# Sparse attention of the odd layer: from per-head items in seven blocks to one block on pairs of heads

## The chip, the cores and the metric

The kernel runs on one core of a Trainium2 chip. Its time is the device time of one execution in microseconds; before the change it is 2824.45 us, the median of three runs (2823.25 to 2824.95). Engines: PE (TensorE), PEld (its weight loads), DVE (VectorE), ACT (ScalarE), POOL (GpSimd), SP (SyncE, which issues most transfers).

## The reference

Two transformer blocks over 256 tokens of width 1024, one after the other; everything is float32. The second block has an even layer (differential attention, state-space mixer, feed-forward) and an odd layer. The odd layer's first half is the place of the change:

```python
q, kc, vc, ksl, vsl, kwn, vwn, gl, cq, ckv, kr = split_cols(h @ od_w_in[i], ODD_SPLITS)
c_out = nsa_attention(q, kc, vc, ksl, vsl, kwn, vwn, gl, ...)     # 8 heads of 64, 2 key groups
d_out = mla_attention(cq, ckv, kr, ...)                           # 4 heads
x = x + concat([c_out, d_out]) @ od_w_out[i]
x = x + moe_swiglu(rms_norm_2(x, od_norm_ffn[i]), ...)            # 8 experts, 2 per token
# inside nsa_attention, for each block of 128 queries and each head:
ck = rope(rms_norm(silu((blocks_of_32(kc) + pos) @ w1[0]) @ w2[0]))   # 15 compressed keys a group
cv = silu((blocks_of_32(vc) + pos) @ w1[1]) @ w2[1]                   # 15 compressed values
o_c = (softmax(mask(q @ ck)) * valid) @ cv
o_s = softmax over the selected blocks' keys (ksl, vsl), causal
o_w = softmax over a window of 512 (kwn, vwn), causal
out = g0 * o_c + g1 * o_s + g2 * o_w                                  # sigmoid gates of gl
```

With 256 tokens there are four blocks of 64 keys, fewer than the 16 that the selection takes, and the window of 512 is wider than the sequence. Both the selected and the window branch are therefore plain causal attention over 256 keys, each on keys and values of its own.

## The kernel before

Tokens lie on the 128 partitions in two tiles (t = 0, 1). Work is written as blocks: inside a block each engine runs its own list of instructions and waits on semaphores, and all engines meet at a block's end. A chained DVE instruction is waited for before the next is issued. `p.ps[i]` is PSUM bank i. A float32 product shows in the records as two PE instructions, a float32 transpose as one.

`linear` (L868) computes the odd layer's projection into `proj` from a stream of 1 MB weight chunks. Beside it POOL runs `nsa_heads` (L1976), norm and rotary embedding of queries and of the two key sets; ACT issues the loads of the compression weights (L270). `nsa` (L1989) then runs block after block:

- `nsa_compress` (L1901): `turn` (L801, transposes on PE, copies by DVE and ACT) of the keys and values to compress, on 64 partitions; then one block for both kinds in turn: position adds on DVE (L1930), 32 products of 64x64 by 30 columns (both groups side by side, L1953), the activation by ACT's exponential and three DVE operations (L1934 to L1936), the second product (L1960); norm and rotary embedding of the compressed keys; a `turn` of them.
- a `turn` of queries and keys: every head's 64 features on partitions 0 to 63.
- `attention` (L1206) on 16 items (head, t) of the compressed branch: scores (L1238), mask added, maximum, scale (L1271, L1273, L1278), exponential with accumulated sum (L1304), validity product (L1282), transpose (L1246), copy (L1312), values (L1256), reciprocal and output (L1289, L1290).
- `attention` on 32 items (branch, head, t); an item has 128 keys for t = 0 and 256 for t = 1, so two items make a cycle.
- a block of the gates: sigmoid, then per tile three products of 512 columns and two sums (L2039 to L2041).

`mla` (L2045) follows, then the output projection, routing and the experts. Another attention of the kernel, `block1_attention` (L1368), works on pairs of heads: two heads' features on partitions 0 to 63 and 64 to 127, scores of the pair into two banks (L1453), maxima on DVE (L1541, L1542), exponentials (L1512), transposes (L1463), copies (L1506), values with a column of ones that yields the sum (L1477), output (L1556 to L1561). Its three calls, on 512, 256 and 512 keys, are in the trace.

## Time and profile before

| | |
|---|---|
| median of 3 runs | 2824.45 us |
| the profiled execution | 2822.43 us, span 2820.7 us |
| PE busy | 2485.3 us (88%) |
| DVE busy | 1855.9 us (66%) |
| ACT busy | 1334.9 us (47%) |
| POOL busy | 204.7 us (7%) |
| granted TensorE clock, mean | 0.910 |
| HBM traffic | 191 GB/s over the span |

Busy times are sums over the span. The granted clock is the share of full speed that the throttle let TensorE have; it is 1.00 at 2.4 GHz and 0.50 at 1.2 GHz, and a stretch with a number between had both. In lines of the timeline the first number is the start in us, the second the time from first start to last end of the merged instructions, and the bracket is the idle time before with what ended it.

### The profile page before, as it was taken

Reading aid. Unit: us, or ns where it says so; the run is one execution under the profiler, and the core shown is the slowest. Engines: PE = TensorE matmul, PEld = TensorE weight load, DVE = VectorE, ACT = ScalarE, POOL = GpSimd, SP = SyncE. Lnnn points to the kernel's source line nnn. Section 1 sums busy time; section 2 is a strip of 40 time slices with the busy share of each in tenths; the row PEclk is TensorE's granted clock in tenths of the full one; section 3 lists DMA queues with packets and bytes.
Section 4 is the critical chain, followed back from the end, with each engine's and each line's share of the span. In section 5 each row is a group of like instructions: output and inputs, shape, how many; then the busy total and the mean of one; then the engine's idle time right before and its main releaser. Section 6 shows DMA issues by size and latency. Waiting matters only on the chain. (4 is left out here: it accounts for less than half of the span.)

```text
span 2820.7 us, 45360 instructions
## 1 busy us (share of the span) xinstructions
PE 2485.3 (88%) x17186; PEld 2233.7 (79%) x17186; DVE 1855.9 (66%) x3132; ACT 1334.9 (47%) x2140; POOL 204.7 (7%) x181
## 2 busy tenths in 40 slices
PE   7888999899978899795389985937899999999998
PEld 5877897789877789794389974626899999999997
DVE  3645555555564555656755552665899999999897
ACT  2343433443344344422144431303677777777776
POOL 0500000000013000071000032000000000000000
PEclk9999999999989999895589985558999999999999
DMA  8604554445531345340045440002799999999995
GB/s 322 253 16 182 214 215 151 165 174 215 194 107 44 132 172 191 126 150 0 0 150 187 172 169 15 1 0 83 287 344 328 342 343 327 341 343 333 329 344 219
DMA packets 82041, 541.75 MB, mean 192 GB/s; under 512 B 9328, under 2 KB 9776, under 8 KB 33840
## 3 DMA queue, kind: packets, MB, share of 16 engines
q1 hardware_dynamic: 79184, 529.57, 50.9%
q10 hardware_dynamic: 2656, 9.40, 0.9%
q8 instruction: 139, 2.28, 0.3%
q14 instruction: 62, 0.51, 0.1%
HBM read 537.88 MB, written 1.05 MB: 191 GB/s over the span
## 5 line engine op out<-in xcount | busy, mean ns | idle before, releaser
L843 PE MATMUL bank<-w_hi,src_hi 128*128 128x256 f32 x2304 | 671.8, 292 | 15.3 <-DVE src_lo L614 4.4
L2471 DVE TENSOR_TENSOR w_lo<-ring,w_hi 128x1024 fp32r<-128x1024 f32 x528 | 637.7, 1221 | 61.3 <-ACT w_hi L2407 41.8
L844 PE MATMUL bank<-w_lo,src_hi 128*128 128x256 f32 x2304 | 653.1, 283 | 0.0
L845 PE MATMUL bank<-w_hi,src_lo 128*128 128x256 f32 x2304 | 652.3, 283 | 0.0
L843 PEld LDWEIGHTS bank<-w_hi,src_hi 128*128 128x128 f32 x2304 | 441.3, 192 | 39.2 <-issue 30.4
L844 PEld LDWEIGHTS bank<-w_lo,src_hi 128*128 128x128 f32 x2304 | 442.0, 192 | 12.1 <-issue 6.7
L845 PEld LDWEIGHTS bank<-w_hi,src_lo 128*128 128x128 f32 x2304 | 442.1, 192 | 0.0
L843 PE MATMUL bank<-src_hi,w_hi 128*128 128x256 f32 x1472 | 426.8, 290 | 12.7 <-DVE w_lo L1150 8.9
L1150 DVE TENSOR_TENSOR w_lo<-ring,w_hi 128x1024 fp32r<-128x1024 f32 x264 | 322.8, 1223 | 169.5 <-ACT w_hi L1087 169.3
L844 PE MATMUL bank<-src_lo,w_hi 128*128 128x256 f32 x1472 | 421.9, 287 | 0.0
L845 PE MATMUL bank<-src_hi,w_lo 128*128 128x256 f32 x1472 | 421.5, 286 | 0.0
L2407 ACT ACTIVATE w_hi<-ring 128x1024 fp32r<-128x1024 f32 x352 | 372.4, 1059 | 102.9 <-PE bank L845 102.0
L1087 ACT ACTIVATE w_hi<-ring 128x1024 fp32r<-128x1024 f32 x264 | 278.3, 1057 | 282.6 <-PE bank L845 282.6
L843 PEld LDWEIGHTS bank<-src_hi,w_hi 128*128 128x128 f32 x1472 | 287.9, 196 | 27.1 <-issue 25.5
L843 PE MATMUL bank<-w_hi,act_hi 128*128 128x512 f32 x704 | 295.1, 419 | 13.0 <-DVE w_lo L1150 11.9
L844 PEld LDWEIGHTS bank<-src_lo,w_hi 128*128 128x128 f32 x1472 | 288.1, 196 | 1.5
L845 PEld LDWEIGHTS bank<-src_hi,w_lo 128*128 128x128 f32 x1472 | 287.8, 196 | 0.0
L845 PE MATMUL bank<-w_hi,act_lo 128*128 128x512 f32 x704 | 279.0, 396 | 0.0
L844 PE MATMUL bank<-w_lo,act_hi 128*128 128x512 f32 x704 | 278.8, 396 | 0.0
L983 DVE TENSOR_TENSOR w_lo<-ring,w_hi 128x1024 fp32r<-128x1024 f32 x120 | 167.6, 1398 | 121.2 <-ACT w_hi L912 120.9
L912 ACT ACTIVATE w_hi<-ring 128x1024 fp32r<-128x1024 f32 x120 | 126.9, 1058 | 216.1 <-PE bank L845 189.7
L2430 ACT ACTIVATE w_hi<-ring 128x1024 fp32r<-128x1024 f32 x176 | 186.9, 1062 | 27.4 <-PE bank L845 24.5
(349 smaller groups left out, 3076.5 us busy)
## 6 DMA issues: line engine op xcount, KB each, us to landing
ring<-in_moe SPq DMA_DIRECT2D x176, 1024.0 KB, 7.2
ring<-in_ffn SPq DMA_DIRECT2D x66, 1536.0 KB, 6.5
ring<-in_moe SPq DMA_DIRECT2D x176, 512.0 KB, 6.8
ring<-in_ffn_ev SPq DMA_DIRECT2D x22, 1536.0 KB, 6.6
oT<-in_w_ada SPq DMA_DIRECT2D x20, 1024.0 KB, 5.4
big<-in_w_ada SPq DMA_DIRECT2D x20, 1024.0 KB, 8.4
ring<-in_w_in SPq DMA_DIRECT2D x18, 1024.0 KB, 6.3
ring<-in_w_out SPq DMA_DIRECT2D x12, 1024.0 KB, 4.9
```

The costliest lines, as they stand in the source:

```text
L843: pe.matmul(out, ah, bh, start=start and i == 0, stop=False, skip_group_check=True)
L844: pe.matmul(out, ah, bl, start=False, stop=False, skip_group_check=True)
L845: mm = pe.matmul(out, al, bh, start=False, stop=stop and i == n - 1, skip_group_check=True)
L912: act.activation(p.wH[:, b, :], p.ring[:, g % RING, (q % 2) * PIECE:(q % 2 + 1) * PIECE], ACT.Copy).then_inc(p.w_hi[b].sem, 1)
L983: ins = dve.tensor_tensor(p.wL[:, b, :], p.ring[:, g % RING, (q % 2) * PIECE:(q % 2 + 1) * PIECE], p.wH[:, b, :].bitcast(F32), ALU.subtract)
L1087: act.activation(p.wH[:, kind, :], piece(c, kind), ACT.Copy).then_inc(p.w_hi[kind].sem, 1)
L1150: dve.tensor_tensor(p.wL[:, kind, :], piece(c, kind), p.wH[:, kind, :].bitcast(F32), ALU.subtract).then_inc(p.w_lo[kind].sem, 1)
L2407: act.activation(sets[k % 2][0][:, half, :], side_piece(k, half), ACT.Copy).then_inc(p.w_hi[half].sem, 1)
L2430: act.activation(sets[m % 2][0][:, DOWN, :], down_piece(m), ACT.Copy).then_inc(p.w_hi[DOWN].sem, 1)
L2471: dve.tensor_tensor(wl, piece, wh.bitcast(F32), ALU.subtract).then_inc(p.w_lo[kind].sem, 1)
```

## The change

`nsa` becomes one block. `turn` and `attention` are not called for it.

- The eight heads are ordered 0, 4, 1, 5, 2, 6, 3, 7, by the host's order of the projection's columns and of the output projection's rows, so that a pair of neighbouring heads has one head of either key group. A transpose of 128 columns gives a pair's queries, the head of group 0 on partitions 0 to 63, that of group 1 on 64 to 127; likewise for keys and for what is compressed. Eight jobs of two transposes do all of it.
- The compression runs for both groups in the two halves of partitions; each group's products have 15 columns and go to a bank of its own. The weights `cmp_w1` and `cmp_w2` are loaded onto both halves (1 MB instead of 512 KB for each kind).
- A unit is (branch, pair) with both query tiles: 8 units. Scores of a unit fill 384 columns in each of two banks; maxima, exponentials and keeps work on both heads and, where shapes allow, both tiles. Values carry a column of ones. The gate is multiplied into the reciprocal; the window branch adds into the selected branch's output.
- The compressed branch is done for all heads at once, in steps placed behind units 0 to 9 on PE and DVE: its keys as a block-diagonal tile (128 by 32), all scores in one bank, one maximum, exponential and normalization over 16 rows of 16, two transposes, and per query tile one product of 128x128 by 512 columns whose result DVE adds to the output.

```diff
-                     ("cmp_valid", NT * N_CMP), ("iota", P)])
+                     ("cmp_valid", NT * N_CMP), ("iota", P), ("cmp_rep", P), ("cmp_block", 8)])
...
-def nsa_compress(p, w1, w2):
...
-    ck, ckT = nsa_compress(p, w1, w2)
-    turn(p, heads_to_T(proj, 0, 8, to(qT, 0)) + heads_to_T(proj, 768, 2, to(kT, 0))
-         + heads_to_T(proj, 1024, 2, to(kT, 2)))
...
-    attention(p, items)
-    items = []
...
-    attention(p, items)
-    gate_exp = p.sig("nsa_gate_exp")
...
+    units = [(w, m) for w in range(2) for m in range(4)]
+    nu = len(units)
+    AT = (0, P, 3 * P)
+    jobs = [("c", 0, 512), ("c", 1, 640), ("k", 0, 768), ("q", 0, 0), ("k", 1, 1024), ("q", 1, P), ("q", 2, 2 * P),
+            ("q", 3, 3 * P)]
+    by_act = (0, 1, 3, 5, 7)
...
+            def hidden(kind):
+                pe.wait_ge(*posed(2 * kind + 2))
+                for i in range(32):
+                    for g in range(2):
+                        r = slice(g * HD, g * HD + HD)
+                        mm = pe.matmul(p.ps[2 * kind + g][r, 0:N_CMP], w1[kind][r, i, :], flat[r, kind, i, :],
+                                       start=i == 0, stop=i == 31)
+                        if i == 31:
+                            mm.then_inc(hid.sem, 1)
...
+            def score(u):
+                w, m = units[u]
+                pe.wait_ge(*job_kept(2 if w == 0 else 4))
+                pe.wait_ge(*job_kept((3, 5, 6, 7)[m]))
+                if u >= 2:
+                    pe.wait_ge(*probs(4 * (u - 1)))
+                else:
+                    pe.wait_ge(*kept(2 * u + 2))
+                for t in range(NT):
+                    for h in range(2):
+                        r = slice(h * HD, h * HD + HD)
+                        mm = pe.matmul(p.ps[2 * (u % 2) + h][:, AT[t]:AT[t + 1]], qT[r, m, t * P:t * P + P],
+                                       kT[r, w, 0:(t + 1) * P], start=True, stop=True)
+                mm.then_inc(scores.sem, 1)
+
+            def turn_probs(u):
+                for h in range(2):
+                    pe.wait_ge(*probs(4 * u + 2 * h + 2))
+                    if u:
+                        pe.wait_ge(*pt_kept(2 * u + h - 1))
+                    for b in range(3):
+                        mm = pe.transpose(p.ps[4 + h][:, b * P:b * P + P], E[:, u % 2, h, b * P:b * P + P], p.ident[:, :])
+                    mm.then_inc(pt_ready.sem, 1)
+
+            def values(u):
+                w, m = units[u]
+                if u == 0:
+                    pe.wait_ge(*v_kept(6))
+                else:
+                    pe.wait_ge(*done(u))
+                for h in range(2):
+                    pe.wait_ge(*pt_kept(2 * u + h + 1))
+                    for t in range(NT):
+                        for b in range(t + 1):
+                            a = AT[t] + b * P
+                            mm = pe.matmul(pv_out()[:, h, t, :], PT[:, u % 2, h, a:a + P], v1[:, b, w, h, :],
+                                           start=b == 0, stop=b == t)
+                mm.then_inc(pv.sem, 1)
+
+            def compressed_step(u):
+                bank = p.ps[7]
+                if u == 3:
+                    pe.wait_ge(*keyed(1))
+                    pe.transpose(bank[:, 0:N_CMP], ck[:, 0, :, :].rearrange("p g d -> p (g d)"), p.ident[0:N_CMP, 0:N_CMP])
+                    pe.matmul(bank[:, 256:384], p.con_at(CON2, "cmp_rep")[0:N_CMP, :],
+                              ck[:, 1, :, :].rearrange("p g d -> p (g d)"), start=True, stop=True).then_inc(spread.sem, 1)
+                if u == 5:
+                    pe.wait_ge(*placed(1))
+                    for t in range(NT):
+                        for m in range(4):
+                            a = (t * 4 + m) * 32
+                            mm = pe.matmul(bank[:, a:a + 32], qT[:, m, t * P:t * P + P], ckbd, start=True, stop=True)
+                    mm.then_inc(c_scores.sem, 1)
+                if u == 8:
+                    pe.wait_ge(*c_probs(1))
+                    for t in range(NT):
+                        mm = pe.transpose(bank[:, t * P:t * P + P], Ec[:, 8 * t:8 * t + 8, :].rearrange("p a n -> p (a n)"),
+                                          p.ident[:, :])
+                    mm.then_inc(c_turned.sem, 1)
+                if u == 9:
+                    pe.wait_ge(*c_kept(1))
+                    for t in range(NT):
+                        if t:
+                            pe.wait_ge(*c_taken(t))
+                        pe.matmul(bank, PTc[:, t * P:t * P + P], Vbd.rearrange("p m g d -> p (m g d)"), start=True,
+                                  stop=True).then_inc(c_out.sem, 1)
+
+            for j in range(4):
+                turn_job(j)
+            hidden(0)
+            for j in range(4, 8):
+                turn_job(j)
+            hidden(1)
+            compressed(0)
+            compressed(1)
+            for u in range(nu + 2):
+                if u < nu:
+                    score(u)
+                if 1 <= u <= nu:
+                    turn_probs(u - 1)
+                if u >= 2:
+                    values(u - 2)
+                compressed_step(u)
...
+            def keep_probs(u):
+                if u >= 2:
+                    act.wait_ge(*pv(u - 1))
+                for h in range(2):
+                    act.wait_ge(*pt_ready(2 * u + h + 1))
+                    act.activation(PT[:, u % 2, h, :], p.ps[4 + h][:, 0:3 * P], ACT.Copy).then_inc(pt_kept.sem, 1)
+
+            def exps(u):
+                st = stat(u)
+                act.wait_ge(*negmax(u + 1))
+                for h in range(2):
+                    for t in range(NT):
+                        act.activation(E[:, u % 2, h, AT[t]:AT[t + 1]], p.ps[2 * (u % 2) + h][:, AT[t]:AT[t + 1]], ACT.Exp,
+                                       bias=st[:, 2 * t + h:2 * t + h + 1], scale=scale).then_inc(probs.sem, 1)
...
+            for j in (0, 1, 3):
+                keep_turned(j)
+            keep_turned(5)
+            hidden_exp(0)
+            keep_turned(7)
+            hidden_exp(1)
+            for u in range(nu + 1):
+                if u >= 1:
+                    keep_probs(u - 1)
+                if u < nu:
+                    exps(u)
+                if u == 6:
+                    act.wait_ge(*c_shift(1))
+                    act.activation(Ec, Sc.rearrange("p t m g n -> p (t m g) n"), ACT.Exp, scale=scale).then_inc(c_exp.sem, 1)
+            act.wait_ge(*c_turned(1))
+            act.activation(PTc, p.ps[7][:, 0:T], ACT.Copy).then_inc(c_kept.sem, 1)
...
+            def maxima(u):
+                st = stat(u)
+                dve.wait_ge(*scores(u + 1))
+                s = p.psum[:, 2 * (u % 2):2 * (u % 2) + 2, 0:3 * P]
+                edge = p.con_at(CON2, "causal", NT)[:, 0, 0:P].unsqueeze(1).broadcast_to([P, 2, P])
+                dve.tensor_tensor(s[:, :, 0:P], s[:, :, 0:P], edge, ALU.add)
+                chain(dve.tensor_tensor(s[:, :, 2 * P:3 * P], s[:, :, 2 * P:3 * P], edge, ALU.add))
+                for t in range(NT):
+                    ins = dve.tensor_reduce(st[:, 2 * t:2 * t + 2], s[:, :, AT[t]:AT[t + 1]], AX_X, ALU.max)
+                chain(ins)
+                dve.tensor_scalar(st[:, 0:4], st[:, 0:4], -scale, None, ALU.mult).then_inc(negmax.sem, 1)
+
+            def keep(u):
+                w, m = units[u]
+                st, o = stat(u), pv_out()
+                dve.wait_ge(*pv(u + 1))
+                r = st[:, 4:8].rearrange("p (h t) -> p h t", h=2)
+                chain(dve.reciprocal(r.unsqueeze(3), o[:, :, :, HD:HD + 1]))
+                chain(dve.tensor_tensor(r, r, gx[:, :, 2 * m:2 * m + 2, 1 + w].rearrange("p t h -> p h t"), ALU.mult))
+                wide = r.unsqueeze(3).broadcast_to([P, 2, NT, HD])
+                if w == 0:
+                    dve.tensor_tensor(out_rows(m), o[:, :, :, 0:HD], wide, ALU.mult).then_inc(done.sem, 1)
+                else:
+                    dve.tensor_tensor(tmp, o[:, :, :, 0:HD], wide, ALU.mult).then_inc(done.sem, 1)
+                    dve.wait_ge(*done(u + 1))
+                    chain(dve.tensor_tensor(out_rows(m), out_rows(m), tmp, ALU.add))
...
+            for j in (2,):
+                keep_turned(j)
+            pose(0)
+            pose(1)
+            for j in (4, 6):
+                keep_turned(j)
+            activate(0)
+            keep_compressed(0)
+            activate(1)
+            keep_compressed(1)
             dve.wait_ge(*gate_exp(1))
-            chain(dve.tensor_scalar(gx, gx, 1.0, None, ALU.add))
-            chain(dve.reciprocal(gx, gx))
-            for t in range(NT):
-                g3 = gx[:, t, :].rearrange("p (h c) -> p h c", c=3)
-                outs = [v.rearrange("p (h d) -> p h d", h=8) for v in (proj[:, t, 0:512], ow[:, 0, t, :], ow[:, 1, t, :])]
-                for c in range(3):
-                    chain(dve.tensor_tensor(outs[c], outs[c], g3[:, :, c:c + 1].broadcast_to([P, 8, HD]), ALU.mult))
-                chain(dve.tensor_tensor(outs[0], outs[0], outs[1], ALU.add))
-                chain(dve.tensor_tensor(outs[0], outs[0], outs[2], ALU.add))
-    gate_exp.passed(1)
+            g = gx.rearrange("p t j c -> p (t j c)")
+            chain(dve.tensor_scalar(g, g, 1.0, None, ALU.add))
+            chain(dve.reciprocal(g, g))
+            for u in range(nu + 2):
+                if u < nu:
+                    maxima(u)
+                if u >= 2:
+                    keep(u - 2)
+                compressed_step(u)
...
-    w1 = [v.rearrange("p a d -> p (a d)")[0:HD, :].rearrange("p (i j) -> p i j", i=32) for v in (p.gates[:], p.ctx[:])]
+    w1 = [v.rearrange("p a d -> p (a d)").rearrange("p (i j) -> p i j", i=32) for v in (p.gates[:], p.ctx[:])]
     free = p.oT[:].rearrange("p k t -> p (k t)")
-    w2 = free[0:HD, 1536:1664].rearrange("p (k j) -> p k j", k=2)
+    w2 = free[:, 1536:1664].rearrange("p (k j) -> p k j", k=2)
...
-    arrays["od_in"] = chunks(a["od_w_in_2"][0], PC)
-    arrays["od_out"] = chunks(a["od_w_out_2"][0], PC)
+    nsa_order = np.array([0, 4, 1, 5, 2, 6, 3, 7])
+    nsa_heads_at = (nsa_order[:, None] * HD + np.arange(HD)[None]).reshape(-1)
+    od_cols, od_rows = np.arange(O_COLS), np.arange(D)
+    od_cols[0:512], od_rows[0:512] = nsa_heads_at, nsa_heads_at
+    od_cols[1280:1304] = 1280 + (nsa_order[:, None] * 3 + np.arange(3)[None]).reshape(-1)
+    arrays["od_in"] = chunks(a["od_w_in_2"][0][:, od_cols], PC)
+    arrays["od_out"] = chunks(a["od_w_out_2"][0][od_rows], PC)
...
-    arrays["cmp_w1"] = np.ascontiguousarray(a["nsa_cmp_w1_2"][0].reshape(2, 32, HD, HD).transpose(2, 0, 1, 3))
-    arrays["cmp_w2"] = np.ascontiguousarray(a["nsa_cmp_w2_2"][0].transpose(1, 0, 2))
+    arrays["cmp_w1"] = np.ascontiguousarray(np.tile(a["nsa_cmp_w1_2"][0].reshape(2, 32, HD, HD).transpose(2, 0, 1, 3),
+                                                      (2, 1, 1, 1)))
+    arrays["cmp_w2"] = np.ascontiguousarray(np.tile(a["nsa_cmp_w2_2"][0].transpose(1, 0, 2), (2, 1, 1)))
```

## Rows read from the trace of the kernel before

**Rows 1.** The page's granted TensorE clock in 40 slices of 70.5 us.

```profile
PEclk9999999999989999895589985558999999999999
```

**Rows 2.** The timeline at the stage's two edges.

```profile
1712.44 0.72 POOL L528 TENSOR_TENSOR proj<-big 128x256 f32<-128x256 f32 x1
1848.23 0.69 DVE L2041 TENSOR_TENSOR proj<-proj,projc 128x512 f32<-128x512 f32 x1
```

**Rows 3.** Stretches of the stage: length, busy time by engine, clock, DMA.

```profile
1712.00:1743.00 31.00, 17.41 (x146) 15.89 (x146) 8.73 (x27) 1.14 (x4) 1.78 (x3) 0.50 0.00 1
1748.70:1774.70 26.00, 23.35 (x80) 16.97 (x80) 15.35 (x96) 8.99 (x48) 0.00 (x0) 0.53 0.00 1
1774.70:1840.70 66.00, 63.68 (x208) 45.60 (x208) 42.00 (x160) 24.52 (x96) 0.00 (x0) 0.50 0.00 1
```

**Rows 4.** The timeline of one kind's compression.

```profile
1716.47 1.94 DVE L1930 TENSOR_TENSOR work<-big,cols 64x240 f32<-64x240 f32 x4 [1.12 <-PEq L805]
1718.46 7.03 PE L1953 MATMUL bank<-work,gates 64*64 64x30 f32 x64 [2.98 <-DVE work L1930]
1726.56 0.60 PE L1960 MATMUL bank<-oT,work 64*15 64x64 f32 x4 [1.06 <-DVE work L1936]
```

**Rows 5.** The timeline of paired attention, 256 keys, full clock.

```profile
497.13 0.70 PE L1453 MATMUL bank<-big 64*128 64x256 f32 x4
497.77 0.66 PE L1463 MATMUL bank<-ident,work 128*128 128x128 f32 x4
498.26 1.00 PE L1477 MATMUL bank<-big 128*128 128x65 f32 x8
499.19 0.70 PE L1453 MATMUL bank<-big 64*128 64x256 f32 x4
```

**Rows 6.** The timeline of the last attention's cycles, half clock.

```profile
1819.85 0.47 PE L1246 MATMUL bank<-ident,work 128*128 128x128 f32 x1
1823.81 0.47 PE L1246 MATMUL bank<-ident,work 128*128 128x128 f32 x1
1823.81 1.03 PEld L1256 LDWEIGHTS bank<-proj,work 128*128 128x128 f32 x4
1824.96 0.79 PE L1238 MATMUL bank<-big 64*128 64x128 f32 x2
1826.62 1.22 PE L1238 MATMUL bank<-big 64*128 64x256 f32 x2
```

**Rows 7.** Groups by line and form: busy us, mean ns, idle before.

```profile
L1541 DVE TENSOR_TENSOR bank<-bank,con 128x256 f32<-128x256 f32 x6 | 2.6, 433 | 2.9 <-PE bank L1453 2.9
L1542 DVE TENSOR_REDUCE att<-bank 128x2 f32<-128x512 f32 x12 | 8.3, 692 | 5.2 <-PE bank L1453 4.3
L1560 DVE RECIPROCAL att<-att 128x2 f32<-128x2 f32 x6 | 1.0, 166 | 0.2
L1512 ACT ACTIVATE work<-bank,att 128x256 f32<-128x256 f32 x24 | 10.1, 477 | 0.2
L1304 ACT ACTIVATE work<-work,stat 128x128 f32<-128x128 f32 x16 | 6.4, 401 | 15.9 <-DVE stat L1278 15.9
L1506 ACT ACTIVATE work<-bank 128x256 f32<-128x256 f32 x12 | 4.1, 381 | 4.8 <-PE bank L1463 4.8
L2085 PE MATMUL bank<-projc,big 128*128 128x512 f32 x8 | 4.7, 671 | 0.0
```

**Rows 8.** A load of compression weights among the DMA issues: KB, us to landing.

```profile
gates<-in_cmp_w ACTq DMA_DIRECT2D x1, 512.0 KB, 5.3
```

**Rows 9.** Stretches of three stages; PEclk is the granted clock.

```profile
485.00:490.00 5.00, 4.68 (x18) 2.52 (x18) 1.72 (x4) 2.47 (x7) 0.20 (x2) 0.50 0.01 2
490.00:495.00 5.00, 4.92 (x38) 3.63 (x34) 2.50 (x8) 3.52 (x11) 0.00 (x0) 0.94 0.00 0
1292.00:1296.00 4.00, 4.00 (x14) 2.84 (x13) 2.66 (x10) 1.37 (x6) 0.00 (x0) 0.50 0.01 4
1745.00:1747.00 2.00, 2.00 (x12) 1.71 (x11) 0.73 (x2) 0.68 (x2) 0.00 (x0) 0.57 0.00 0
```

More of the change, by code:

```diff
@@ new lines, in job_kept, with job_dst, stat, pv_out @@
+    def job_kept(j):
+        if j in by_act:
+            return kept_a(1 + by_act.index(j))
+        return kept_v(1 + [i for i in range(len(jobs)) if i not in by_act].index(j))
+    def job_dst(j):
+        kind, i, a = jobs[j]
+        return {"c": cT, "k": kT, "q": qT}[kind][:, i, :]
+    def stat(u):
+        return p.att[:, u % 4, :]
+    def pv_out():
+        return p.ps[6][:, 0:260].rearrange("p (h t d) -> p h t d", h=2, t=NT)
+    def out_rows(m):
+        return proj[:, :, m * P:m * P + P].rearrange("p t (h d) -> p h t d", h=2)
@@ new lines, in exps, with hidden_exp @@
+            def exps(u):
[5 more added lines that the diff above has]
+                                       bias=st[:, 2 * t + h:2 * t + h + 1], scale=scale).then_inc(probs.sem, 1)
+            def hidden_exp(kind):
+                for g in range(2):
+                    r = slice(g * HD, g * HD + HD)
+                    act.wait_ge(*hid(2 * kind + g + 1))
+                    if kind:
+                        act.wait_ge(*act_done(g + 1))
+                    act.activation(hsb[r, 0, :], p.ps[2 * kind + g][r, 0:N_CMP], ACT.Exp, scale=-1.0).then_inc(act_exp.sem, 1)
@@ new lines, in activate @@
+            def activate(kind):
+                dve.wait_ge(*act_exp(2 * kind + 2))
+                if kind:
+                    dve.wait_ge(*out_ready(2))
+                chain(dve.tensor_scalar(hsb[:, 0, :], hsb[:, 0, :], 1.0, None, ALU.add))
+                chain(dve.reciprocal(hsb[:, 1, :], hsb[:, 0, :]))
+                for g in range(2):
+                    r = slice(g * HD, g * HD + HD)
+                    dve.tensor_tensor(hsb[r, 2, :], hsb[r, 1, :], p.ps[2 * kind + g][r, 0:N_CMP],
+                                      ALU.mult).then_inc(act_done.sem, 1)
```

243 lines of the change are left out of this document (149 added, 94 removed).

## The prediction

> **What bounds the kernel now.** I read the slices with the clock row first [rows 1]: two places of the span hold a half-rate TensorE clock, and the second, the 25th to 27th slice (1692 to 1904 us), holds the stage that the change rewrites. Every engine meets at the block boundaries around the sparse attention, so what the stage loses or gains moves the end one for one. The timeline gives its edges [rows 2]: GpSimd finishes the rotary work at 1712.44 + 0.72 = 1713.16 and DVE the last gated sum at 1848.23 + 0.69 = 1848.92. The stage is **135.8 us** long. The table of stretches [rows 3] splits it: compression 30 (from 1713.16), then transposes to 1748.7 (5.7), compressed attention 26, selected and window attention 66, gates 8.2 to its end. In the 66 us PE is busy for 63.68 at a granted clock of 0.50, the 1.2 GHz level: PE-bound at half rate. In compression nobody is busy for long; PE, ACT and DVE hand one small tile around.
>
> **Part 1, the compression.** Before, each kind takes 1.94 us of position adds, 7.03 us for 64 matmul records (32 products of 30 columns, each in two records) and 0.60 us for the second product [rows 4], strictly one after the other. After, both key groups lie in the two halves of the partitions: position adds are four on 128 partitions at 1.94/4 = 0.49 us, but the products become 64 per kind with 15 columns. If products in different row halves of the array run together, a kind stays at 7.0 us. The paired score records bear on it [rows 5]: unpaired at half rate, two records take 0.79 with 128 columns and 1.22 with 256 [rows 6], so 128 columns cost 0.215 a record and 256 cost 0.43, at full rate 0.215. Four such records one after the other would be 0.86 us before the next group starts; in the paired program at full rate the next group starts after 0.64 (497.13 to 497.77), drain included [rows 5]. So row halves do overlap. Bounds: 7.0 as now, 14.1 if each record keeps its 7.03/64 = 0.11 us; 3.5 if the clock is full. I take 7.0.
> The Trainium skill, "TensorEngine Tiling (Array Packing)", Performance Considerations, speaks against this edit: a product of one column costs as much as one of sixty, so a small dimension should not be cut further for the sake of tiles; by it a record doesn't get cheaper with 15 columns, and the gain rests on the overlap alone. The same page's Overview promises the overlap for 64x64 tiles; the trace here shows it for 64x128 only.
> Order on the path from 1713.16: 0.4 to start (as 1713.56 before), four jobs of two transposes (0.49/4 = 0.12 each at full rate, 497.77 to 498.26 [rows 5]; I take 0.21 to 0.24 at half); job 2 copied by DVE at 2.5; two adds to 3.5; first hidden product 3.65 to 10.6; eight more transposes to 12.5; second hidden product to 19.5; second-layer product 0.6, two copies, four small DVE operations 0.95 (an estimate at 0.17 to 0.43 each, the ends of [rows 7]'s small and 256-element work), second-layer product of the other kind 0.6. First scores at **22.3**, where the old program reached its first compressed score 35.5 after the start (1748.7 [rows 3]). The transposes of queries and keys, 5.7 us with their own block before, are among the sixteen of this sum.
>
> **Part 2, sixteen pair-steps become eight units, with 32 items' small operations gone.** The old 32 items ran as 16 cycles of 3.96 us [rows 6], 1819.85 to 1823.81. A unit holds two such cycles. On PE nothing is saved in transposes (6) and value records (12, bound by weight loads: 1.03 us for four at half rate, 0.233 apart when the last is taken as 0.33), only the scores pair up. At half rate: scores 2x0.213 + 2x0.427 = 1.28, transposes 6x0.21 = 1.3, values 12x0.233 = 2.8, together 5.4. The same prices make 3.3 of the old cycle of 3.96, so four switches between scores and the rest took 0.6; I give the two of a unit, with two row halves to drain, as much: **6.0 us**, against 7.92. At full rate half of it and 0.35 for the switches: **3.1**. The same program shape on 256 keys runs at 2.06 us a unit without extra job at full rate [rows 5]; my unit is one and a half times it: 3.1.
> DVE in a unit, from rows of the same operations on the same memory [rows 7]: two mask adds of 256 in PSUM at 0.43, maxima of 256 and 512 elements 0.43 and 0.69, a scale 0.16, with 0.04 between chained ones 2.2 us; then reciprocal 0.16, gate 0.16 (estimates by the smallest row), output 256 elements 0.43, and for the window half a further add 0.42: 0.85 or 1.3. Eight maxima 17.6, keeps 4x0.85 + 4x1.3 = 8.6.
> ACT: four exponentials (0.48 for 256 elements, 0.40 for 128, partly overlapped), two copies of 384, above the 0.38 of 256: 1.6 + 1.0 = 2.6 us a unit. So at full clock DVE is the last, at half clock PE.
>
> **Part 3, the compressed branch.** 26 us of its own become steps inside the units. DVE, by the same per-element rows: norm sum 1.1, norm 0.6, rotary 1.1, block-diagonal tiles 1.1, mask and shift 1.5, weights 1.8, two adds of 512 at 0.69: **8.5 us**, all in DVE's queue, with maxima and keeps queued behind. PE gets 16 records of weight load 0.233, 0.8 for the spreading, two transposes, and two products of 512 columns; such a record takes 0.67 in the mean [rows 7]; two by columns as above are 1.7 at half rate, 0.9 at full. PE sum 8.5 at half rate.
> **Part 4, gates.** 8.2 us of gate products (1840.7 to 1848.9) go; their factor sits in the units (in the keeps above). GpSimd's value copies lie beside the transposes, under 3 us with 20 of cover. The two 512 KB weight loads become 1 MB each; the first lands in 5.3 us, issued in the projection's front, some 60 us before its use [rows 8]; at that rate another 10 us of queue, hidden by the projection's 45 us of products: nothing, and a few us at most if the projection's last chunks were short of cover. The host's column order and the 68 KB of extra constants cost nothing on the chip's path.
>
> **Sum.** First scores at 22.3 and done at 23.9; DVE's own work 17.6 + 8.6 + 8.5 = 34.7; exposed at the end: last values behind the last-but-one keep 1.5, hand-overs 0.5, second 512-column product behind the first add 1.1, boundary 0.4, another 0.6 for the copy of the turned weights: 4.1. That is 62.7 if DVE never waited. It will wait while the first units fill (values of unit 0 are behind scores 2 and transposes 1), for which I take 3, and for PE while the clock is at half, 3.5. Stage **69.2**, saving 66.6. 2822.43 (span 2820.7 and 1.7 around it) - 66.6 = 2755.8; the median of the runs lies 2.0 above the profiled one: **2758**.
> **The clock.** The row says [rows 9]: paired attention began at 0.50 with PE busy 4.68 of 5 us, and was at 0.94 and 1.00 in the next stretches; unpaired attention of another layer stayed at 0.50 with PE busy 4.00 of 4.00. The new units have the proportions of the first. But at full clock DVE holds them, PE would be busy 3.1 of some 4.3 us, thinner than the 4.92 of 5 there; it may fall again, hence the 3.5 us above, between 0 and 14.
> The row of stretch 1745 to 1747 shows the clock rising with nothing but transposes on PE [rows 9]. The Trainium skill, "TensorE: Matmul & The Clock Gate", Part 4, says that transposes don't bring the clock up; by it the opening and the units' transposes would keep half rate and the half-rate sum holds. The trace disagrees with it, so it gets only the chance of the next case.
>
> **Rivals.** (a) Half rate throughout: PE 8x6.0 + 8.5 = 56.5 after 22.3, and fill and tail of 5: 84, time 2772. For: 0.50 held for all of the old attention. Against: rows 9 for the paired form. 20%. (b) The hidden products don't overlap: 7.1 more for each kind, at the clock of the forecast: 83.4, time 2772. For: never seen for this tile; 10%. (c) Full clock from the hidden products on: 7 less there and no waits for PE: 59, time 2748. For: twice the rows active; against: 0.50 through all of 14 us of the old ones with PE busy nearly throughout. 12%. (d) Slower: units don't overlap, each running its whole chain because one value bank and in-order queues tie them (values wait for the keep before, keeps sit behind compressed steps). Chain at half rate: 1.6 + 2.2 + 1.6 + 1.65 + 1.0 + 2.9 + 1.1, compressed steps 1.1 on DVE and 1.1 on PE, eight hand-overs 0.7: 14.9; 22.3 + 8x14.9 + 3 = 144.5, 8.7 slower, 2833. It decides from 13.8 us a unit on. Against: in [rows 5] scores, transposes and values of three successive units follow each other within 2.06 us in the same order of issue. 3%. (e) The program isn't what runs (the old branch still called): none of it in the diff; under 1%. The forecast's own case, 2753 to 2766, has 54%.
>
> **Range and chances.** 2746 to 2776 takes in (a), (b), (c). Faster by over 0.2% (5.6 us, what a measurement of this kernel can tell): 0.96; within: 0.01; slower: 0.03.
>
> **What would show it.** Stage length by its edges; PE records at the hidden line per kind in 7 us (Part 1) or 14; first scores 22 us after GpSimd's last; start-to-start of units 3.5 to 4.5 us with DVE busy nearly throughout (Part 2), or 6 with PE busy and clock 0.50 (a); DVE of compressed steps 8.5 in all; the two 512-column products as the last PE work. Wrong would be a stage beyond 90 us, or a change of more than 3 us outside it.

## The result, and the profile after

The changed kernel takes **2761.3 us** (median of 4 runs, 2758.1 to 2762.93) beside 2824.7 us of the kernel before on the same chip (2823.25 to 2825.49): a ratio of 0.9775, with a 95% interval of 0.9758 to 0.9792. The forecast was 2758, 2746 to 2776. A second set of 4 runs gave 2762.29 us and 0.9785 (0.9768 to 0.9801).

The slices of the page after, to be laid beside [rows 1]: engines first, then the granted clock of TensorE. The 25th to 27th slice (1656 to 1863 us) still has the low clock digits, with less of it.

```profile
PE   7888999989987899989279987766999999999998
DVE  3645555555555555564865553654999899899997
PEclk9899999999988999997579988667999999999999
```

The edges of the stage, from two timelines (start, duration, engine, line, operation), to be laid beside [rows 2]:

```profile
1713.43 0.72 POOL L528 TENSOR_TENSOR proj<-big 128x256 f32<-128x256 f32 x1
...
1780.21 0.69 DVE L2267 TENSOR_TENSOR proj<-proj,bank 128x512 f32<-128x512 f32 x1 [2.17 <-PE bank L2078]
```

1714.15 to 1780.90 is **66.75 us**, where it was 135.76. The stage gives 69.0 us. But the two profiled executions differ by 59.5 (2822.43 and 2762.93; the second is the slowest of its four, so the medians lie 63.4 apart). Of the other 9.5, 1.0 lies around the span (1.8 us before, 2.8 after), 1.0 ahead of the stage, and **7.4 behind the stage**: 971.8 us from its end to the end of the span before, 979.2 after. I followed this through common marks: from the stage's end to the first transpose of the latent attention 46.4 and 46.6; from there to the output projection 24.34 and **28.99**; on to the MoE 61.28 and 61.32; the MoE up to its last addition 834.9 and **837.5**. Nothing of these two parts is in the diff. The mixture-of-experts part (the experts of the reference) is called MoE here. The table of stretches shows what is different in the first (start and end, length, busy time and count for PE, PEld, DVE, ACT, POOL, then the granted clock). One line of before:

```profile
1895.30:1919.64 24.34, 19.43 (x103) 14.49 (x104) 13.51 (x47) 9.47 (x32) 0.00 (x0) 0.90 0.00 1
```

and the same 103 records after, whole and cut where the clock changes:

```profile
1827.51:1856.50 28.99, 25.63 (x103) 18.80 (x104) 13.88 (x47) 9.48 (x32) 0.00 (x0) 0.67 0.00 1
...
1827.51:1833.00 5.49, 5.46 (x26) 5.03 (x26) 2.53 (x6) 1.99 (x6) 0.00 (x0) 0.50 0.01 3
1833.00:1836.40 3.40, 2.39 (x11) 1.22 (x10) 1.31 (x5) 0.80 (x3) 0.00 (x0) 1.00 0.00 0
1836.40:1850.10 13.70, 13.69 (x44) 9.67 (x45) 7.12 (x27) 4.06 (x16) 0.00 (x0) 0.50 0.00 0
1850.10:1856.50 6.40, 4.09 (x26) 2.88 (x26) 2.92 (x11) 2.63 (x9) 0.00 (x0) 1.00 0.01 1
```

The clock rises 5.5 us after the first transpose, falls again after a stretch in which PE was busy for 2.39 of 3.40 us, and stays down for 13.7 us with PE busy throughout. Before, it rose 5.0 us after the first transpose and held. That is 4.65 us on a path that PE bounds.

Inside the stage, the stretches of after:

```profile
1714.15:1735.36 21.21, 18.44 (x280) 17.20 (x280) 4.91 (x17) 2.76 (x10) 1.09 (x6) 0.50 0.01 2
1735.36:1745.76 10.40, 8.68 (x51) 6.42 (x49) 8.27 (x26) 5.16 (x14) 0.70 (x1) 0.57 0.01 2
1745.76:1757.56 11.80, 11.36 (x98) 9.77 (x97) 10.21 (x34) 6.91 (x19) 0.00 (x0) 1.00 0.01 1
1757.56:1762.12 4.56, 4.56 (x28) 3.84 (x27) 2.08 (x6) 2.84 (x9) 0.00 (x0) 0.63 0.00 0
1762.12:1768.11 5.99, 3.44 (x30) 2.86 (x29) 5.47 (x17) 2.64 (x8) 0.00 (x0) 1.00 0.00 0
1768.11:1780.90 12.79, 10.63 (x35) 6.95 (x33) 5.52 (x16) 1.52 (x4) 0.00 (x0) 0.50 0.00 1
```

The opening ran at half rate, the units from the third on at 1.00 but for one dip of 3.4 us to 0.50 (1757.9 to 1761.3), the tail at half rate again, after a stretch in which PE was busy for only 3.44 of 5.99 us. The opening and the end on PE's timeline:

```profile
1717.54 7.01 PE L2002 MATMUL bank<-big,gates 64*64 64x15 f32 x128 [1.01 <-DVE big L2160]
...
1726.38 7.01 PE L2002 MATMUL bank<-big,ctx_res 64*64 64x15 f32 x128
...
1735.36 2.93 PE L2025 MATMUL bank<-big 64*128 64x128 f32 x16
...
1772.61 2.82 PE L2049 MATMUL bank<-big,work 128*128 128x65 f32 x12 [0.51 <-DVE big L2203]
1775.23 2.02 PE L2078 MATMUL bank<-big 128*128 128x512 f32 x2
1778.09 2.08 PE L2078 MATMUL bank<-big 128*128 128x512 f32 x2 [0.85 <-DVE proj L2267]
```

L2002 is the hidden product of a kind, 128 records for 7.01 us (before 64 of 30 columns for 7.03 [rows 4]); L2025 the scores, first at 21.2 us after the start; L2078 the two 512-column products of the compressed branch, the second behind VectorE's addition out of the same bank. Two things I could not tell from this trace: whether the time lost behind the stage is where the clock's changes happen to fall, or something that the change leaves behind; and what within the stage its parts cost.

### The profile page after: what moved, and what is told of

Same layout as the page of the kernel before. It is cut to its first block and busy times, and to the rows that moved or that the text cites. A ratio compares the mean times of both kernels' runs of the same rounds, so it can differ in the third digit from the quotient of the medians.

```text
span 2760.1 us, 44941 instructions
## 1 busy us (share of the span) xinstructions
PE 2444.1 (89%) x17241; PEld 2207.3 (80%) x17241; DVE 1816.7 (66%) x2949; ACT 1320.8 (48%) x2048; POOL 204.6 (7%) x187
```

## The experiments

All are edits of the changed kernel unless said. The part is the latent attention from its first transpose to the output projection, 24.34 us before and 28.99 after. Ratios are to the kernel before, timed beside each run.

**1. Filling TensorE's gaps behind the stage** (`warm_mla`).

```
+def keep_warm(p, pe, bank, n):
+    for _ in range(n):
+        pe.matmul(p.ps[bank], p.ident[:, :], p.con_at(CON2, "causal"), start=True, stop=True)
 # mla, first block, PE
+            keep_warm(p, pe, 7, 6)
 # mla, second block, PE, behind the up-projections
+            pe.wait_ge(*kept(1))
+            keep_warm(p, pe, 7, 18)
```

> The changed kernel with 24 products of 512 columns that nobody reads, put on TensorE where it stands idle in the latent attention behind the stage: 6 while VectorE takes the first norms (1781.2 to 1791.7) and 18 behind the last copy of the up-projections (1805.3 to 1827.5). Theory (the time lost behind the stage is clock): without such a gap the granted clock stays at 1.0 from about 1785 on and through the attention up to 1860, the window 1826 to 1860 shrinks by 4 to 6 us, what follows is unchanged, and the run is 4 to 7 us under the changed kernel: ratio to before 0.9755 less 0.002, so 0.9750 to 0.9762 where the changed kernel has 0.9775. Rival (something the change itself leaves behind, a late load or a buffer, holds the later parts): clock up, but the start of the MoE does not move by more than 1 us. Second rival (the added products only delay the transposes queued behind them): slower by 1 to 3 us.

2755.43 us, ratio 0.9765 (0.9749 to 0.9782), against 0.9775 and 0.9785 for the changed kernel: its interval holds the first and ends just under the second. The stretches (those of the second filling, then the whole of transposes and attention):

```profile
1801.50:1823.40 21.90, 16.56 (x38) 6.79 (x37) 15.67 (x21) 0.00 (x0) 4.91 (x3) 1.00 0.00 0
...
1824.66:1853.68 29.02, 25.64 (x103) 18.80 (x104) 13.89 (x47) 9.46 (x31) 0.00 (x0) 0.67 0.00 1
```

The second filling did go with a clock of 1.00, but it ran out 1.3 us before the transposes, the clock fell at that point, and the part took 29.02 us at 0.67 as ever. (The first filling didn't hold it: the clock was at 0.50 again from 1789.2 to 1796.1.) The forecast of 4 to 6 us there failed, and the start of the MoE didn't move against the stage's end. That is the first rival's number, but its condition, a high clock in the attention, never came, so the run speaks neither for it nor against the theory. The profiled MoE was 2.0 us shorter (835.4), which no theory had promised; why, stands behind experiment 8.

**2. Filling the gap ahead of the stage** (`warm_open`).

```
 # linear of the input projection, PE, at its end
+            if warm:
+                pe.wait_ge(*taken(4))
+                keep_warm(p, pe, 6, warm)      # warm = 15
```

> The changed kernel with 15 unread products of 512 columns on TensorE between the end of the input projection (its last product, about 1699) and the start of the stage (1714.15), where it stands idle. Theory: the half rate of the opening is the state the idle 15 us leave; with the clock at 1.0 at 1714 the 128 hidden products of a kind take 3.5 us in place of 7.0 and the stage shortens by 7 to 9 us, to 58 to 60 us; the run comes out 5 to 9 us under the changed kernel. Rival: the 15-column products count as no load, the clock falls to 0.5 within 5 us of the opening whatever came before; the stage gains 2 us at most, and the run is within 2 us of the changed kernel. Second rival: as in the theory, but the stage then waits for VectorE and ScalarE (copies, adds, activations between the products), so that of 7 us only 3 or 4 are seen.

2765.95 us, ratio 0.9806 (0.9790 to 0.9823): *slower* than the changed kernel (2762.29 and 2761.3), by some 4 us in the times and 6 to 9 in the ratios (0.9785 and 0.9775), whose intervals overlap a little. PE's timeline, then the stretches:

```profile
1698.21 13.11 PE L870 MATMUL bank<-con,ident 128*128 128x512 f32 x30
...
1715.48 6.96 PE L2010 MATMUL bank<-big,gates 64*64 64x15 f32 x128 [1.23 <-DVE big L2168]
```

```profile
1700.00:1715.60 15.60, 12.51 (x39) 5.75 (x39) 1.52 (x4) 1.28 (x4) 12.49 (x28) 1.00 0.00 1
1715.60:1722.30 6.70, 6.70 (x128) 6.70 (x128) 0.76 (x2) 0.00 (x0) 0.00 (x0) 0.50 0.01 2
1733.00:1739.50 6.50, 4.74 (x32) 3.25 (x34) 5.17 (x18) 2.27 (x6) 0.70 (x1) 0.76 0.00 0
1739.50:1760.00 20.50, 19.66 (x93) 16.32 (x90) 12.10 (x38) 8.84 (x25) 0.00 (x0) 0.50 0.00 1
```

The stage opened at 1.00; the clock fell 2.8 us in, behind gaps of 1.9 and 1.2 us on PE and 0.1 us behind the first hidden product, and the hidden products, back to back, then ran at 0.50 to their end. So the rival holds in this: a clock that is up at the start of the opening doesn't last through it. Whether the gaps or the products brought it down, this run can't tell. The earlier opening then moved the units against the clock: it rose at 1736.1, fell at 1739.5 and stayed at 0.50 to 1760.0, through units that the changed kernel ran at 1.00. The stage grew by 6.8 us, which the rival had not foreseen.

**3. Without the compressed branch** (`no_cmp`): every `compressed_step` of PE, the steps from the third on of VectorE, and ScalarE's two operations for them are left out.

> The changed kernel without the compressed branch behind the normalised compressed keys: no spread, scores, softmax, turn and products of it on any engine, so the output has no compressed part. My reading of the trace (VectorE was busy for 36.5 of 66.8 us, so the branch sits in its gaps; only what comes behind the eighth unit is on the path): the stage ends 6 to 9 us earlier, nearly all of it behind the last unit's values, and the unit periods of 3.4 to 4.6 us change by less than 0.5 us each. Rival (the forecast: at the full clock VectorE is the last, with 8.5 us of the branch on it): the units come closer as well, by 0.5 to 1 us each, and the stage ends 11 to 15 us earlier.

2747.25 us in one run. The stage shrinks by **10.7 us** to 56.0: 6.7 from the first scores to the last value product (39.7 to 33.0), 4.1 behind it. That lies between the two numbers and nearer to the forecast's. What was left out is 5.75 us of VectorE's work (36.46 to 30.71 in the stage), as the forecast's rows for it had it (1.1 + 1.5 + 1.8 + 1.4); the keys' norm and rotary work stay in. A stretch of its units:

```profile
1743.40:1755.90 12.50, 12.35 (x107) 10.21 (x106) 10.90 (x32) 8.92 (x25) 0.00 (x0) 1.00 0.01 1
```

Four units in 12.5 us, 3.1 each, as forecast for PE at full rate; but it is PE that is full (12.35 of 12.50), VectorE has 2.7 us a unit and waits. With the branch in, the units from the fourth on stand 3.4 to 4.7 us apart. Not all of that is the branch's: one of them, 4.56 us, is the row 1757.56:1762.12 above, with the dip of the clock in it and PE busy throughout. Here the clock didn't dip, and the stage has 35.5 us at half rate where the changed kernel has 46.3. So the 10.7 us are the branch with its effect on the clock.

**4. Which halves of the array let two products overlap** (`same_rows`, `same_tile`).

```
 # same_rows: operands of both groups and heads from partitions 0 to 63
-  pe.matmul(p.ps[2 * kind + g][r, 0:N_CMP], w1[kind][r, i, :], flat[r, kind, i, :], ...
+  pe.matmul(p.ps[2 * kind + g][r, 0:N_CMP], w1[kind][0:HD, i, :], flat[0:HD, kind, i, :], ...
 # and in score(u)
-  r = slice(h * HD, h * HD + HD)
+  r = slice(0, HD)
 # same_tile: hidden products alone, outputs too
+  pe.matmul(p.ps[2 * kind + g][0:HD, 0:N_CMP], w1[kind][0:HD, i, :], flat[0:HD, kind, i, :], ...
```

> The changed kernel in which both heads' score products, and both groups' hidden products, read their operands from partitions 0 to 63 (group 0's data; the second head's and group's values are wrong), all else alike. Theory (two products run side by side because they stand on different row halves of the array): the hidden products of a kind go from 7.0 to 14.0 us, the scores of a unit take 1.5 to 2 times as long, and the stage grows by 14 to 20 us. Rival (a product's weight load and issue set 0.11 us a record, and row halves have nothing to do with it, or column halves alone suffice): the hidden products stay at 7.0 us and the stage within 2 us.

One run, 2778.95 us, stage 86.5 (19.8 longer). By form, at PE; and the same of the changed kernel behind it:

```profile
L2025 PE MATMUL bank<-big 64*128 64x256 f32 x32 | 15.3, 631 | 0.0
L2025 PE MATMUL bank<-big 64*128 64x128 f32 x32 | 9.6, 453 | 0.0
L2002 PE MATMUL bank<-big,gates 64*64 64x15 f32 x128 | 7.0, 263 | 1.0 <-DVE big L2160 1.0
```

```profile
L2025 PE MATMUL bank<-big 64*128 64x256 f32 x32 | 6.6, 503 | 0.0
L2025 PE MATMUL bank<-big 64*128 64x128 f32 x32 | 4.7, 379 | 0.0
```

The scores double, the hidden products stay. The two sets of score rows differ in clock as well, so the test is the first sixteen score records, at half rate in both: they start within 2.30 us in the changed kernel and 4.85 here. The clock was at 0.50 in the whole stage here, with the unpaired products on 64 rows, as in nearly all of the old attention [rows 3]. Neither theory had this mixture, hence:

> The changed kernel in which the hidden products of both groups read partitions 0 to 63 and write partitions 0 to 63 of their two banks, one and the same quarter of the array; the second group's values are wrong. With row halves alone shared they stayed at 6.75 us a kind (52.7 ns a record). Theory P (the two groups run side by side, by their column halves then): sharing both makes a kind 13.5 us. Theory Q (nothing runs side by side here: a product's price is its columns, 15 against 30 of the kernel before, at 0.11 us for 30): a kind stays at 6.75 us and the stage at 66.7.

2777.13 us in one run, the stage 13.7 longer, and each kind twice as long:

```profile
L2002 PE MATMUL bank<-big,gates 64*64 64x15 f32 x128 | 13.8, 263 | 1.0 <-DVE big L2160 1.0
```

Theory P. Two products run side by side when they differ in the column half alone (hidden products with shared rows and different columns: 7.0) or in the row half alone (the scores, which take all columns: 2.30 us against 4.85); sharing both makes them queue. Hidden products that differ in rows alone weren't run. And a record of 15 columns, alone, costs 13.8/128 = 0.108 us at half rate, as much as one of 30 (0.11 [rows 4]): fewer columns gave nothing, the overlap gave all. The Trainium skill, "TensorEngine Tiling (Array Packing)", Performance Considerations, says that a product of one column takes as long as one of sixty, and here the trace agrees.

**5. Where the latent attention falls against the clock** (`late_half`, `late_two`).

```
 # mla, VectorE, behind its last norm
+            chain(dve.tensor_tensor(p.work[:, 0:512], p.work[:, 0:512], p.work[:, 0:512], ALU.add))
```

> The changed kernel with one needless VectorE addition of 128x512 (0.47 us and a turn of the queue, 0.5 in all) behind the last norm of the latent attention, so that TensorE's transposes and attention start 0.5 us later. Theory A (where that part falls against the instants at which the clock is switched decides its rate): of the first transpose to the next rise of the clock it was 5.0 us before the change and 5.5 to 5.9 us in the five kernels behind it, with one fall to 0.5 for 13.7 us in each of the five and none before; moved by 0.5 us the rise comes 5.0 us behind the first transpose again, the part runs at 1.0, takes 24.3 us in place of 29.0, and the kernel with more work in it is 3.5 to 4.5 us faster than the changed one (about 2757). Theory B (the part is slower for another reason that the change leaves behind, so always): 29.0 us again, and 0.5 us slower in all.

> As late_half with two additions, of 128x1024 and 128x768, together 1.7 us. Theory A: the rise comes 3.8 us behind the first transpose; the part's length differs from 29.0 us, and I expect the short form, 23 to 25 us, since the window before the rise no longer holds the wait for the softmax. Theory B: 29.0 us, and 1.7 us slower in all.

late_half: **2755.84 us**, ratio 0.9768 (0.9752 to 0.9785), by the profile 3.4 us less from the stage's start to the end of the span, with 0.8 us more work in it (0.76 and not the 0.5 of the text). The transposes and the attention, of late_half and of late_two:

```profile
1825.68:1850.39 24.71, 19.80 (x100) 14.79 (x101) 13.58 (x48) 9.56 (x31) 0.00 (x0) 0.85 0.00 1
```

```profile
1830.33:1853.83 23.50, 18.59 (x103) 13.67 (x104) 13.52 (x47) 9.47 (x31) 0.00 (x0) 0.93 0.00 1
```

A delay shortens the part behind it by 4.3 and 5.5 us. Theory A, in both. (The whole kernel's interval in late_half still holds the changed kernel's ratio; the case for it is the part.) late_two as a whole took 2760.93 us in one run: its 2.3 us of additions eat part of it, and its end behind the last addition of the MoE was 2.0 us longer.

**6. The compressed branch one unit earlier** (`early_cmp`).

```
 # PE: scores at u == 4, turn at 7, products at 8;  VectorE: placed at 3, softmax at 5 and 6, added at 8
 # ScalarE: exponential at 5, copy of the turned weights behind the last unit's exponentials
```

> The changed kernel with the compressed branch one unit earlier from its spread on: placed at unit 3, scores at 4, softmax at 5 and 6, turned at 7, products and additions at 8, so that they stand ahead of the last unit's values and not behind them. Theory (what the two 512-column products and their additions cost is their place at the end, 6.2 us from the last value product to the end of the stage where 2.4 do without them): the end moves by 3 to 4 us, TensorE's and VectorE's gaps ahead of the last values take the products in, the stage is 63 us. Rival: they cost TensorE the same 4.1 us at half rate wherever they stand, since it is the bound there; the stage stays within 1 us of 66.7. The time of the run may differ by some us more either way, by where the parts behind fall against the clock.

2760.73 us, ratio 0.9783 (0.9767 to 0.9799); the stage is 0.6 us shorter (66.2). My theory fell, the rival holds: from PE's timeline, the products now stand ahead of the last values, where PE works at half rate just the same.

```profile
1771.15 2.02 PE L2078 MATMUL bank<-big 128*128 128x512 f32 x2
1774.02 2.08 PE L2078 MATMUL bank<-big 128*128 128x512 f32 x2 [0.86 <-DVE proj L2270]
1775.89 2.66 PE L2049 MATMUL bank<-big,work 128*128 128x65 f32 x12
```

The clock is not the same in the two stages: here the dip is missing, and 42.3 us are at half rate for 46.3. So the 0.6 is not the edit's alone, and what the place does by itself isn't shown closer than that.

**7. A bank of its own for the second product** (`two_banks`).

```
-                        if t:
-                            pe.wait_ge(*c_taken(t))
-                        pe.matmul(bank, PTc...
+                        pe.matmul((bank, p.ps[0])[t], PTc...
 # VectorE adds the second from p.ps[0]
```

> The changed kernel with the second of the two 512-column products at the end of the stage in a bank of its own (one that the sixth unit's scores have left), so that it needn't wait for VectorE's addition out of the first. Theory A: the 0.85 us gap ahead of that product goes, the stage is 0.9 us shorter (65.8), the first transpose of the latent attention comes 0.9 us earlier against the instants of the clock, so that the next rise comes 3.0 us behind it; that is near the 3.3 us of the kernel with 1.7 us added, and the part takes 23 to 25 us and not 29. Whole: 4.5 to 6.5 us under the changed kernel, of which only 0.9 are the edit's. Theory B (the short part of the two delayed kernels came from the delay and not from where it put the part): 29 us, and 0.9 us faster in all.

> The changed kernel once more, beside the others of this call. Every theory: 0.9775 times the kernel before, within 0.0015; its latent attention 29.0 us in the profiled run.

**2755.67 us**, ratio 0.9762 (0.9746 to 0.9778); the changed kernel beside it 2762.29: 6.6 us, with each of its four runs under each of the other's four. The stage gives 1.4 (it is 65.4) and the latent attention 5.7, while 0.7 are lost between them (47.4 us from the stage's end to the first transpose, for 46.6):

```profile
1773.80 3.52 PE L2076 MATMUL bank<-big 128*128 128x512 f32 x4
```

```profile
1825.38:1848.69 23.31, 18.39 (x103) 13.48 (x104) 13.52 (x47) 9.47 (x31) 0.00 (x0) 0.94 0.01 2
```

This was forecast from the place of the rise alone, and came: the rise stands 2.8 us behind the first transpose. after_again was as said, 28.97 us for that part. In this measurement the version is faster than both kernels of the case.

**8. The same shift in the kernel before** (`late_before`, `late_before2`): VectorE additions behind the last norm there, of 1024, 1024 and 800 columns, then of 1024, 1024 and 128.

> The kernel before the change with 2.75 us of needless VectorE additions behind the last norm of the latent attention. Theory A: the rise of the clock, 5.0 us behind the first transpose in that kernel, comes 2.25 us and then again 5.7 us behind it, as in the changed kernel; the part loses its 24.3 us and takes 29, and the kernel is 6.5 to 8 us slower for 2.75 us of work. Theory B (the kernel before runs that part fast by its nature): 24.3 us, and 2.5 to 3 us slower.

2828.78 us, ratio 1.0020 (1.0010 to 1.0030). It decided nothing: the additions took 3.56 us, and the clock rose 4.9 us behind the first transpose, as before (5.0), for a part of 24.71 us. I had sized them from the 958 ns of a group that mixes 512 and 1024 columns; on the timeline (here of late_two) it is

```profile
1827.55 1.22 DVE L2351 TENSOR_TENSOR work<-work 128x1024 f32<-128x1024 f32 x1
```

> The kernel before the change with needless VectorE additions of 128x1024, 128x1024 and 128x128 behind the last norm of the latent attention. The trace of the run with three larger ones shows 1.26 us a turn of 1024 columns, and not the 0.96 that I had taken from a mean over two forms: it was 3.56 us later in all, which put the rise of the clock 4.9 us behind the first transpose, where it was (5.0), and so could not tell the theories apart. Here it is 2.7 us. Theory A: the rise comes 5.6 to 5.9 us behind the first transpose, as in the changed kernel, the part takes 29 us in place of 24.3, and the kernel is 6.5 to 8.5 us slower than before. Theory B (the kernel before runs that part fast by its nature): 24.3 us, 2.5 to 3.5 us slower.

2827.29 us, ratio 1.0016 (1.0006 to 1.0026). The rise came 5.6 us behind the first transpose and the clock did fall again, but for 3.4 us only:

```profile
1896.41:1921.88 25.47, 21.18 (x103) 15.51 (x104) 13.51 (x47) 9.47 (x32) 0.00 (x0) 0.82 0.00 1
```

1.1 us lost, not 4.7. Theory A is right in that the shift brings the fall, wrong in its size. (The profiled execution, 2824.32 us, is the fastest of ten that go up to 2830.64; what the part took in the others isn't known.)

Together, the transposes and the attention of the latent part, with nothing in them edited:

```
kernel           clock rises, us behind     part, us   clock
                 the first transpose
two_banks        2.8                        23.31      0.94
late_two         3.2                        23.50      0.93
late_half        4.8                        24.71      0.85
late_before      4.9                        24.71      0.85
before           5.0                        24.34      0.90
after_again      5.5                        28.97      0.67
after            5.5                        28.99      0.67
warm_mla         5.5                        29.02      0.67
late_before2     5.6                        25.47      0.82
```

warm_open, no_cmp, same_rows, same_tile and early_cmp had the rise at 5.5 to 5.9 too, and parts of 29.0 to 29.2 us. Up to 5.0 the clock holds for at least 17 us; from 5.5 on it falls after 3.4. Why it then stays down for 13.7 us in seven kernels and 3.4 in late_before2, the runs don't say.

The MoE's share stands in the same traces. From its first product to the first transpose behind it, before and after:

```profile
1982.06:1996.55 14.49, 11.46 (x80) 11.10 (x80) 8.73 (x11) 8.88 (x11) 0.00 (x0) 0.88 0.25 83
```

```profile
1918.96:1936.03 17.07, 14.09 (x81) 13.78 (x81) 8.92 (x11) 8.78 (x11) 0.00 (x0) 0.72 0.30 106
```

These 2.58 us are all of the difference, and they go with the clock: before, it rose 3.6 us behind that first product and stayed up; after, it was at 0.50 for 6.2 us and once more from 9.6 to 13.0, 9.6 us in all. The fourteen profiles order themselves by this time at half rate, with nothing edited in the MoE: with 3.0 to 3.6 us it takes 834.4 to 834.9 us (before, same_rows, late_before2), with 6.2 it takes 835.4 to 835.6 (warm_mla, warm_open, no_cmp, early_cmp), with 9.2 to 9.6 it takes 837.0 to 837.5 (the other seven). No run was made to move it alone.

## Why the prediction was right, point by point

- **Part 1, the compression**: right in number and in reason. A kind takes 7.01 us, first scores came at 21.2 us (forecast 22.3). Rival (b), no overlap, is refuted by the changed trace and priced by same_tile: 6.8 more a kind, where 7.1 was written. "Row halves do overlap" was half of it; the column halves do it too.
- **Part 2, the units**: PE's 3.1 us at full rate was exact (no_cmp). "At full clock DVE is the last" was wrong: VectorE has 2.7 us a unit without the branch and stands idle beside a full PE. I had 2.2 + 0.85 for it, with a gap after every operation; the trace has 2.0 + 0.8. The sign named for the forecast's own case, DVE busy nearly throughout, failed too: behind the opening it is busy for 31.6 of 45.5 us, PE for 38.7.
- **Part 3, the compressed branch**: forecast 8.5 us on VectorE's path, of which no_cmp takes out 5.75; the stage is 10.7 shorter. The work was sized rightly, its price wasn't: the steps pull the units from 3.1 to 3.4–4.7 us, by way of waits and of the clock as well as work, and 4.1 us lie behind the last values.
- **Part 4, gates**: gone, and the loads hidden: the time ahead of the stage moved by 1.0 us, which is there 167 us into the program already; in after_again the stage starts 1.4 us earlier than before.
- **Sum**: 66.75 for 69.2, a saving of 69.0 for 66.6. The terms cancelled in part: VectorE's 34.7 us behind the opening were 31.6, and its idle time from the first scores on was 14.0 where 12.2 were allowed (1.6, 3, 3.5 and the 4.1 at the end). The 4.1 can't be checked by itself: it holds waits alone, and the 5.5 us behind the last value product (1775.43 to 1780.90) hold two additions of 0.7, all at a clock that had fallen to half again at 1768. So the sum came out near by a split that was wrong: it took VectorE for the last engine and added PE's half-rate time as a small wait.
- **The clock**: up in the units, as expected from the paired form [rows 9], but neither in the opening (c) nor throughout at half (a). The opening's half rate isn't left over from the idle time ahead of it: a clock that was up didn't last (warm_open).
- **"A change of more than 3 us outside it"** would be wrong, said the text, and that failed: +7.4 behind the stage. The step that is missing from the sum is that shortening a stage moves what follows against the changes of the clock. 4.65 of the 7.4 stand in the latent attention and are undone by a delay of 0.8 us (late_half, −4.3) or a shortening of 1.4 (two_banks, −5.7): shown. The MoE's 2.6 go with the clock in its first 13 us in all fourteen traces, without a run that moves them alone.

The whole came out 3.3 us above the forecast; the stage was 2.4 better, and the parts behind it worse. That it came so near is partly luck: between the profiled executions the saving is 59.5 for 66.6, and the 2.0 us that the forecast added for the median were in truth 1.6 the other way.

## What to carry to other kernels

A saving in one stage can be partly given back in unchanged code behind it: compare the two traces by marks behind the edit, with the granted clock per stretch, before looking for a cause in the edit. When small changes of opposite sign (a little more work, a little less) both win several us, the cause may be where a part falls, and the gain may not survive the next edit; time such versions over again when anything ahead of them changes. For two small fp32 products to share the array it was enough that they differ in one half, columns (64x64) or rows (64x128); going from 30 columns to 15 alone gave nothing.

## What was not expected of the hardware

- The clock's changes stand fixed against the program: it fell ahead of the stage 11.2 to 11.3 us before its first transpose in all thirteen profiles that leave that gap as it is, and in the latent attention the rise and the fall of after and after_again agree to 0.03 us, though their stages start 2.4 us apart. So the loss came again in both profiled executions of the kernel; the mean clock of all its eight runs lies between 0.918 and 0.920.
- Needless work shortened what follows it: 0.76 us of additions took 4.3 us off the latent attention (late_half).
- The hidden products, records of 64x64 tiles back to back with PE busy 6.70 of 6.70 us, did not bring the clock up in 14 us (warm_open, and the same in the changed kernel), where transposes alone had done so [rows 9]. Nor did scores that share a row half (same_rows, 0.50 in the whole stage).
